# Two of the expert chunks of a decoder step are loaded by seven transfers each in place of one

## What is computed

```
def expert_block(args):
    tok, e = args
    xb = x_pad[tok]
    h = jnp.einsum('rd,df->rf', xb, w_gate_up[e]) + b_gate_up[e]
    gate = jnp.minimum(h[:, :D_FF], SWIGLU_LIMIT)
    up = jnp.clip(h[:, D_FF:], -SWIGLU_LIMIT, SWIGLU_LIMIT)
    glu = gate * jax.nn.sigmoid(gate * SWIGLU_ALPHA)
    return jnp.einsum('rf,fd->rd', (up + 1.0) * glu, w_down[e]) + b_down[e]
```

## Time and profile before

| | us |
|---|---|
| median of 3 runs | 1219.21 |
| lowest and highest | 1219.15 and 1220.6 |
| the profiled execution | 1219.81 |
| its span, first to last instruction | 1217.9 |
| TensorE busy in the span | 1157.6 (95%) |
| VectorE, ScalarE, GpSimd busy | 301.4, 142.8, 45.1 |

### The profile page before, as it was taken

The page is one execution under the profiler, slowest core; times in us unless marked ns, Lnnn a source line. Parts: engine busy times, 40 slices in busy tenths (PEclk is TensorE's granted clock), DMA queues, the critical chain, the costliest instruction groups (busy, mean ns, idle before and its releaser), DMA issues.

```text
span 1217.9 us, 14231 instructions
## 1 busy us (share of the span) xinstructions
PE 1157.6 (95%) x5863; PEld 612.4 (50%) x5863; DVE 301.4 (25%) x701; ACT 142.8 (12%) x284; POOL 45.1 (4%) x80
## 2 busy tenths in 40 slices
PE   8999999999999999999998998988998989899986
PEld 7888678876434444343434343524343434353332
DVE  4333311223123122222212122211221212122212
ACT  2122111002110100001010101010101000001112
POOL 3032310000000000000000000000000000000000
PEclk9999999999999999999999999999999999999999
DMA  9752776483999999999999999999999999999995
GB/s 320 241 207 87 248 253 226 138 337 151 416 425 427 418 429 430 428 431 430 430 429 428 429 425 434 426 433 424 434 425 431 428 430 429 434 425 429 426 420 209
DMA packets 59595, 451.31 MB, mean 371 GB/s; under 512 B 3745, under 2 KB 34765, under 8 KB 40064
## 3 DMA queue, kind: packets, MB, share of 16 engines
q1 hardware_dynamic: 56288, 439.60, 87.0%
q0 software_dynamic: 2896, 10.11, 2.5%
q10 hardware_dynamic: 344, 0.61, 0.1%
HBM read 444.46 MB, written 6.08 MB: 370 GB/s over the span
## 4 chain that ended last, share of the span: by engine, by line
PE 73%; DMA 23%; DVE 2%; issue 1%; SPq 1%; ACT 0%; DVEq 0%
PE psum L1035 29%; DMA ring<-in_w_gate_up 20%; PE psum L971 19%; PE psum L1046 8%; PE psum L1115 7%; DMA ring<-in_w_down 3%; PE psum L1143 2%; PE psum L1105 1%; PE psum L1144 1%; PE psum L1036 1%; SPq L556 1%; PE psum L837 0%; PE psum L852 0%; DMA consts<-in_consts 0%; DVE normed L1910 0%
## 5 line engine op out<-in xcount | busy, mean ns | idle before, releaser
L1035 PE MATMUL psum<-ring,x_T 128*64 128x512 f32 x992 | 456.9, 609 | 26.2 <-DMA ring<-in_w_gate_up 19.1
L1036 PE MATMUL psum<-ring,x_T 128*64 128x512 f32 x992 | 457.0, 610 | 0.0
L1035 PEld LDWEIGHTS psum<-ring,x_T 128*64 128x64 f32 x992 | 131.2, 139 | 283.9 <-issue 271.9
L1046 PE MATMUL psum<-ring,act_T 128*64 128x512 f32 x960 | 212.6, 595 | 15.9 <-DMA ring<-in_w_down 15.9
L971 PE MATMUL psum<-ring 128*128 128x264 f32 (+1 forms) x768 | 182.4, 392 | 1.2 <-ACT ring L1375 0.6
L971 PEld LDWEIGHTS psum<-ring 128*128 128x128 f32 x768 | 143.1, 190 | 31.3 <-issue 4.2
L1046 PEld LDWEIGHTS psum<-ring,act_T 128*64 128x64 f32 x960 | 68.8, 137 | 146.7 <-issue 132.9
L1036 PEld LDWEIGHTS psum<-ring,x_T 128*64 128x64 f32 x992 | 131.4, 140 | 0.0
L1823 DVE TENSOR_TENSOR hidden<-psum,params 128x512 f32<-128x512 f32 x32 | 22.1, 691 | 310.0 <-PE psum L1105 310.0
L1115 PE MATMUL psum<-one_hot,normed 128*128 128x128 f32 x768 | 91.5, 276 | 0.6 <-DVE one_hot L1723 0.6
L1115 PEld LDWEIGHTS psum<-one_hot,normed 128*128 128x128 f32 x768 | 88.5, 192 | 5.0 <-issue 5.0
(11 more groups left out here) (263 smaller groups left out, 667.0 us busy)
## 6 DMA issues: line engine op xcount, KB each, us to landing
ring<-in_w_gate_up SPq DMA_DIRECT2D x44, 4096.0 KB, 30.6
ring<-in_w_down SPq DMA_DIRECT2D x56, 2048.0 KB, 32.8
ring<-in_w_gate_up SPq DMA_DIRECT2D x40, 2048.0 KB, 15.9
ring<-in_w_in SPq DMA_DIRECT2D x21, 1024.0 KB, 5.4
ring<-in_w_down SPq DMA_DIRECT2D x12, 1024.0 KB, 29.1
out<-ring POOLq DMA_DIRECT2D x9, 512.0 KB, 4.5
ring<-in_state_ret POOLq DMA_DIRECT2D x8, 512.0 KB, 7.0
ring<-in_w_ret_branch SPq DMA_DIRECT2D x4, 1024.0 KB, 5.0
```

The lines of the kernel that those rows point to most:

```text
L1035: mm(psum[0:CAP, 2 * j + n], x, gate, start=first, stop=final)
L1036: last = mm(psum[CAP:P, 2 * j + n], x, up, start=first, stop=final)
L1046: last = mm(psum[j * CAP:(j + 1) * CAP, 4 + n], hidden[:, j, 4 * h + i], w, start=h == 0 and i == 0, stop=h == 1 and i == 3)
```

## The change

A table EIGHTS names two chunks, (pair 1, chunk 4) and (pair 13, chunk 4), both the first down chunk of their pair's twelve. For these `load_chunk` issues six transfers of eight rows, rows 0 to 47, and then one of the 80 rows 48 to 127. All seven add 16 to the slot's semaphore, and the counts that PE waits for follow. The bytes, their places in the ring and HBM, and the order of the chunks stay.

```
+EIGHTS = {(1, KC): 6, (NPAIR - 3, KC): 6}
+
+
+def transfers(p, c):
+
+    return EIGHTS.get((p, c), 0) + 1
+
...
-            PER_PASS[_s] = PER_PASS.get(_s, 0) + 1
+            PER_PASS[_s] = PER_PASS.get(_s, 0) + transfers(_p, _c)
         LANDED[_p, _c] = PER_PASS[_s]
...
-            PER_LOOP[signal(_p, _c)] += 1
+            PER_LOOP[signal(_p, _c)] += transfers(_p, _c)
...
             if p0 < NPAIR - 1:
                 src = dn_w[bass.ds(e, 1), :, h, :].rearrange("a p f -> p (a f)")
-                sp.dma_start(slot(s), src).then_inc(expert_in[s], 16)
+                alone = 8 * (transfers(p0, c) - 1)
+                for a in range(0, alone, 8):
+
+                    sp.dma_start(slot(s)[a:a + 8], src[a:a + 8]).then_inc(expert_in[s], 16)
+                sp.dma_start(slot(s)[alone:P], src[alone:P]).then_inc(expert_in[s], 16)
                 return
```

## The result

The changed kernel takes 1247.15 us (median of four runs, 1244.99 to 1249.14) against 1219.35 us: ratio 1.0224, 95% interval 1.0212 to 1.0236. That is 27.8 us slower. The forecast was slower by 16.3 us, 1235.5, and the time lies 1.2 us above the top of its range.

A forecast was written before the change was run, and what follows sets the result against it. The DMA weight stream, gapless from 311 us, was taken to decide the end. Two split chunks at +10.5 us each gave +20.9, less 4.6 us of head start = +16.3 on 1219.2: 1235.5 us, range 1216.8 to 1246.

The forecast's parts named there:

- +20.5 us: Both split chunks: eight adjacent rows in two SBUF ports, 2.4 us per 128 KB, 12.6 us a chunk, less head start.
- +10.5 us for the first split: Per split chunk, loaded half of the engines: six eight-row transfers at 2.05 us plus 5 x 0.61, minus 4.89.
- the loaded half: In each split chunk, eight engines carry 11 rows and the other eight 5, in place of 8 and 8.
- Less the 4.6 us that this half was ahead.: Stream's end: the early eight engines finish some 4.6 us before the late eight; subtracted from +20.9 to give +16.3 us.
- 5 x 0.61: The 80-row transfer of a split chunk: five rows for each engine at full speed, 0.61 us a row, 3.05 us.
- The high end of the price: Tail of the y_sample store, 51 GB/s at share 0.18: 2.57 us per eight-row transfer, +22.6 us in all.
- y_sample's 2.25: Final store of eight 4 KB rows: 0.366 us a row against 0.163, so 1.37 us for a 16 KB row.
- The mark for the end: Stream's end in the profile after: a half share lasting longer than 4 us, now because the other eight are early.
- the balance at full speed: Rival: eight-row transfers run at full speed and the engine halves meet at the end; 1217.4 to 1218.3 us, chance 0.22.
- the late half being the loaded one: Rival: extra rows fall on the late engines; 1222.9 us without slow rows, 1240 with them; chance 0.10.
- Rows spread over 16 engines: Rival: eight-row transfers use all 16 engines, nothing shifts, only narrow transfers' price, +11 us, 1230 us; chance 0.05.
- The rows pull apart: Rival: leading engines leave the crowd, an eight-row transfer's price falls from 2.05 to near 0.9 us; 1221.7 us, chance 0.08.

The follow-up runs named there:

- only_first: The changed kernel with its split (six adjacent eights and 80 rows) only in pair 1's chunk, not in pair 13's: 1231.68 us, ratio 1.0095.
- own_ports: The changed kernel with both chunks split into ten strided transfers of 16 or eight rows (rows 32-95, 0-31, then 96-127): 1229.54 us, ratio 1.0081.
- two_parts: The changed kernel with the six eight-row transfers made one again, so both chunks split into 48 and 80 rows: 1237.93 us, ratio 1.0147.

## Why the prediction was wrong

Right:
- **The bound.** The stream decides from 311 us on, and a delay at 314 us is not hidden by PE's lead. only_first shows it alone: 10.8 us lost at the first split, 12.5 us at the end.
- **The direction, and that rows on few places are slow.** An eight-row transfer was taken at 2.05 us and took 1.84. The Trainium skill, SBUF — State Buffer, Door 1: The DMA port swizzle, has the grouping that the runs bear out in all but the quarter speed, though the text used it for the eights alone and its +20.5 us keeps the same 4.6 us of head start.
- **PE did not stall at the first split**, and SP's extra issues are not what costs: own_ports issues ten transfers where the changed kernel has seven, and lost 2.8 us there against 10.7.
- **Marks.** Rate well under 427 at a share near 1.0: 150 and 1.00. The split chunk's last landing at 332.1 us, 21 us after its first issue at 310.95; over 20 was said. Waits near 1035: 5.96 us at 1044 and 7.42 us at 1061. PE's first wait came at 447 us; near 480 was said, from a lead that shrinks evenly.

Right by luck:
- **+10.5 us for the first split.** That was the forecast for the loaded half, with 1.83 us gained by the other. 10.7 us is what the mean engine lost. By the landings behind the split (340.0 before, 347.9 after, and 0.9 us for the earlier start) the loaded eight are 11.8 us late and the other eight 9.1. For the loaded eight, 6 x 1.84 + 5 x 1.20 - 4.89 = 12.2: the eights were 1.3 us cheaper than forecast and the 80 rows 3 us dearer.

Wrong, by the size of the error:
- **"Less the 4.6 us that this half was ahead."** This is the term that failed. It takes the other half to run at 0.61 us a row while the loaded half waits, and all of the loaded half to be early. Neither was so. The other half was on the 80 rows, at 1.84 us a row while the eights ran beside it, and lost 9.1 us at the first split; the head start is one over that half, and it was held up almost as long. And two of the loaded eight were late engines: they had no head start at all, and end the stream, +3.2 us. Together 4.6 + 3.2 = 7.8 of the 10.3 us that the sum of 16.3 is short of 26.6.
- **"5 x 0.61" for the 80 rows, and both chunks at one price.** The 80 rows run at half speed, 215 GB/s in two_parts. In the first split the sum came out even so; the second split cost 12.7 us, 2.2 more than the 10.5 forecast. With the first, 10.7 + 12.7 = 23.4 against 20.9, the remaining 2.5 us of the error.
- **The high end of the price, 131 KB / 51 GB/s = 2.57 us.** It divides by a rate at which the engines were 0.18 busy. For each busy engine that store moved 51 / (0.18 x 16) = 17.7 GB/s, a factor of 1.5 on 26.6, which is below y_sample's 2.25. So 2.05, chosen from below that end, owes its nearness to 1.84 in part to luck.
- **The mark for the end**, a half share longer than 4 us: it was 0.55 for 4 us and then two engines for more.

Of the rivals, the balance at full speed was the furthest off. The one nearest in time was the late half being the loaded one (1240, chance 0.10): it had rightly no head start, but of the loaded eight only two were late. "Rows spread over 16 engines" falls, since each eight-row transfer has eight landings. "The rows pull apart" falls too: the price of a row did not drop from transfer to transfer, it stood at 1.83 to 1.88 us. The range was too short above because no case in it put a price on the 80 rows, or let the slow rows hold up engines that don't carry them.

## What to carry to other kernels

Splitting a full-width load by rows is not neutral even where each part keeps all 16 engines busy: look at which rows of SBUF the engines write at the same moment. Two thirds of the loss here came with a cut into 48 and 80 rows, and a cut into 64 and 64 costs 5 to 11 us by its place. A DMA share of 1.00 tells that the engines are occupied, not that they move bytes: read GB/s beside it. And engines that are ahead in a saturated stream were no reserve for extra rows here: the rows need a free place to be written to, the engines beside them are held up too, and the eight that got the rows were not the eight that were ahead.

None of the kernels here came below the one before. A whole transfer of 128 rows was the fastest shape measured, and no experiment pointed to a better one.

## What the hardware showed beyond that

- Four transfers of 256 KB, each 16 rows with a stride of four, ran at 398 GB/s behind each other: small transfers are cheap in a full queue if their rows don't meet.
- In a saturated stream the same cut costs twice as much late (11.6 us from 1010 us on and 13.4 us from 1070 us on, as the second and third split of their kernels) as early (6.6 us at 311 us).
- Transfers of eight adjacent rows slowed the whole queue: rows on engines that carry none of them took 1.83 us too, in place of 0.61. With spread rows the same eights ran at 23.5 GB/s an engine.
- The slow rows slow more than themselves. At the second split of after the stretch below full rate lasts from about 1028 to 1055 us, 27 us for a chunk of 4.9 us, and the gate_up chunks ahead of it and the down chunks behind it are in it: PE waits for both kinds there.
